# A third landing slot for the modulation blocks, and later first index scores, in a two-layer hybrid decoder trunk

## The chip, the cores and the metric

The kernel runs on one core of a Trainium2 chip. It is one hand-ordered program: every engine (TensorE = PE, VectorE = DVE, ScalarE = ACT, GpSimd = POOL, and SyncE = SP, which here issues nearly all DMAs) executes its own list of instructions in the order written, and semaphores tie the lists together. The metric is the device time of one execution in microseconds (us), lower is better.

## The reference

Two layers, 512 tokens (SEQ) of width 1024 (D). What matters for the change, cut to its core:

```python
c_act = silu(c)
for l in range(2):
    mod = c_act @ w_ada[l] + b_ada[l]                  # (1, 6144): six vectors of 1024
    sh1, sc1, gt1, sh2, sc2, gt2 = split(mod, 6)
    h = rmsnorm(x, g_norm1[l]) * (1 + sc1) + sh1
    proj = h @ w_in[l]                                 # 16 groups of columns, four attention groups A, B, C, D
    # group D: an indexer scores all keys for each query, the top 128 are attended
    #   score[q, k] = sum over 8 heads of wi[q, head] * relu(qi[q, head] . ki[k])
    x = x + gt1 * (four attentions @ w_out[l])
    h = rmsnorm(x, g_norm2[l]) * (1 + sc2) + sh2
    x = x + gt2 * mixture_of_experts(h)                # 16 experts, 2 per token
return rmsnorm(x, g_final)
```

All of it is float32. `w_ada[l]` is 1024 x 6144. Its first 2048 columns (sh1, sc1) are needed before the layer, the other 4096 (gt1, sh2, sc2, gt2) only after the attention.

## The kernel before, in words

**Modulation.** The 4096 later columns of `w_ada[l]` are read in 16 *blocks* of 128 rows x 2048 columns (1 MB), block b by `load_ada(b)` (L1485) on SP's queue into `ada_slot(b)` (L323), one of two slots at the end of `wbuf`, chosen by b % 2. DVE multiplies block b with one column of silu(c) and adds it to a running sum by `ada_step(b)` (L670; L675 for the first block of a sum, L678 for the others). Blocks 0 to 7 sum in `qB`, 8 to 15 in `kB`. `load_ada(b)` waits until DVE has used block b - 2. PE then adds the partitions up (`sum_mods`, L1091). In layer 0 blocks 16 to 23 follow during the output projection, for the next layer.

**Projection.** `w_in` comes in seven column *chunks* (CHUNKS, L32) through two slots of `wbuf`. Chunk n may be loaded (`load_in`, L1481) only when the last PE job that reads chunk n - 2 has filled its bank: chunk 2 waits for `kiwi`, chunk 3 for `kvD`, chunk 4 for `ckv`. A PE *job* is one output tile (8 matmuls of 512 columns; the profile counts 16 records for it) into one of six PSUM banks, taken round robin in the order of `plan` (L66). A job may begin when the bank's job six places earlier has been drained by ACT or DVE. Jobs of chunk 0 are qi0, qi1, kiwi, of chunk 1 qD0, qD1, kvD, of chunk 2 cq0, cq1, ckv, of chunk 3 qA0, qA1, kA0.

**Index scores.** The indexer runs for query tiles i = 1, 2, 3 (tile 0 needs none). For tile i, PE computes eight small products ("idx" jobs, `host`, L1144: four ahead of each of two projection jobs), ACT takes each through Relu into one of three `relu` buffers (`relus`, L495), DVE multiplies by `wi` and sums into `score` (`index_sums`, L723, L730 and L732), and `top(i)` (L736) takes the 128 largest in 16 rounds of MAX8 and MATCH_REPLACE8 and writes the mask `selmask`. The fourth Relu of a tile cannot run before DVE has consumed the first. Everything DVE does is in one order: blocks 0 to 9, `wi`, scores and top of tile 1, blocks 10 to 15, scores of tile 2, and so on.

**SP's order** in layer 0: chunk 1, blocks 0 and 1, five constant tables, blocks 2 and 3, the 17 small tables of the layer (`load_small`, L1420), blocks 4 to 8, chunk 2, blocks 9 to 11, chunk 3, blocks 12 to 15, chunks 4 to 6. Layer 1 has the same order without tables; its small tables were loaded in layer 0.

**Value tiles.** `vA`, `vB`, `vC`, `vD` (L157) hold the value rows of the attention groups. vA and vB are written from the jobs vA and vB on, well behind the last block of a layer.

## Time and profile before

| | us |
|---|---|
| median of 3 runs | 1188.87 (1188.62 to 1189.19) |
| the profiled execution | 1189.58, its span 1187.7 |
| PE busy | 1037.6 (87%) |
| DVE busy | 597.4 (50%) |
| ACT busy | 357.5 (30%) |
| DMA | 238.33 MB, mean 201 GB/s |

Read it in stages: in each of the two layers come projections with the indexer (about 39 to 216 us in layer 0, 616 to 785 us in layer 1), then attention, the output projection and the experts. The change touches only the first of these stages. A busy share of 87% for PE is an average; what a wait costs is read at its place. Times inside the trace count from the span's start; "clock" is the share of full speed that TensorE was granted.

### The profile page before, as it was taken

Reading aid. Unit: us, or ns where it says so; the run is one execution under the profiler, and the core shown is the slowest. Engines: PE = TensorE matmul, PEld = TensorE weight load, DVE = VectorE, ACT = ScalarE, POOL = GpSimd, SP = SyncE. Lnnn points to the kernel's source line nnn. Section 1 sums busy time; section 2 is a strip of 40 time slices with the busy share of each in tenths; the row PEclk is TensorE's granted clock in tenths of the full one; section 3 lists DMA queues with packets and bytes.
Section 4 is the critical chain, followed back from the end, with each engine's and each line's share of the span. In section 5 each row is a group of like instructions: output and inputs, shape, how many; then the busy total and the mean of one; then the engine's idle time right before and its main releaser. Section 6 shows DMA issues by size and latency. Waiting matters only on the chain.

```text
span 1187.7 us, 15253 instructions
## 1 busy us (share of the span) xinstructions
PE 1037.6 (87%) x5471; PEld 712.7 (60%) x5471; DVE 597.4 (50%) x1356; ACT 357.5 (30%) x809; POOL 94.3 (8%) x115
## 2 busy tenths in 40 slices
PE   3968999999997699999829899999999859999980
PEld 0423365788554687887624336568865558788860
DVE  1438688766555223223165769786732532322326
ACT  2121233666212223223032122366621222322312
POOL 3000102000000101000020010200000010110002
PEclk8888999999998699999959999999999969999995
DMA  9884425400246499999588451130000549999955
GB/s 364 267 286 146 171 73 172 201 1 1 106 160 222 109 353 360 372 370 356 192 290 295 165 196 54 36 142 1 1 1 36 178 141 348 356 377 369 354 192 212
DMA packets 141317, 238.33 MB, mean 201 GB/s; under 512 B 31322, under 2 KB 111690, under 8 KB 134990
## 3 DMA queue, kind: packets, MB, share of 16 engines
q1 hardware_dynamic: 134356, 212.52, 51.0%
q0 software_dynamic: 6912, 25.17, 5.7%
q8 instruction: 29, 0.48, 0.2%
q14 instruction: 20, 0.16, 0.0%
HBM read 214.57 MB, written 27.26 MB: 204 GB/s over the span
## 4 chain that ended last, share of the span: by engine, by line
PE 72%; DVE 11%; DMA 11%; issue 2%; SPq 2%; ACT 2%; POOL 1%; POOLq 0%; DVEq 0%; ACTq 0%
PE bank L1068 64%; DMA wbuf<-in_w_ada 7%; PE bank L1085 5%; PE bank L1353 2%; DMA bada<-in_b_ada 2%; DVE qB L678 2%; DVE tring L742 1%; DVE x L1046 1%; DVE kB L678 1%; DVE small L741 1%; DMA hT<-y_rows,ints 1%; DMA tok<-norm_rows,ints 1%; SPq L1449 1%; DVE tring L732 1%; DMA y_rows<-tok 1%
## 5 line engine op out<-in xcount | busy, mean ns | idle before, releaser
L1068 PE MATMUL bank<-hT,wbuf 128*128 128x128 f32 (+2 forms) x2560 | 463.1, 343 | 3.7 <-ACT pring L502 2.9
L1068 PEld LDWEIGHTS bank<-hT,wbuf 128*128 128x128 f32 (+1 forms) x2560 | 331.0, 194 | 137.3 <-issue 124.2
L1068 PE MATMUL bank<-wbuf,hT 128*128 128x512 f32 (+2 forms) x512 | 155.9, 462 | 1.4 <-ACT hT L474 1.4
L1068 PEld LDWEIGHTS bank<-wbuf,hT 128*128 128x128 f32 x512 | 86.5, 191 | 61.9 <-issue 56.4
L1018 DVE TENSOR_TENSOR tring<-bank,tring 128x256 f32<-128x256 f32 x32 | 13.6, 425 | 218.5 <-ACT tring L620 218.5
L1068 PE MATMUL bank<-wbuf,tring 128*128 128x512 f32 x256 | 114.8, 592 | 0.0
L564 ACT ACTIVATE tring<-tring,small 128x384 f32<-128x384 f32 (+5 forms) x128 | 69.3, 541 | 51.4 <-DVE small L813 50.0
L620 ACT ACTIVATE tring<-bank 128x256 f32<-128x256 f32 x32 | 12.3, 384 | 235.9 <-PE bank L1068 235.9
L1068 PEld LDWEIGHTS bank<-wbuf,tring 128*128 128x128 f32 x256 | 46.3, 190 | 46.9 <-issue 46.9
L1025 DVE TENSOR_TENSOR tok<-bank,gtB 128x512 f32<-128x512 f32 x64 | 44.3, 692 | 45.9 <-PE bank L1068 45.9
L678 DVE SCALAR_TENSOR_TENSOR qB<-wbuf,small,qB 128x2048 f32<-128x2048 f32 x21 | 49.3, 2350 | 25.7 <-DMA wbuf<-in_w_ada 25.3
L582 ACT ACTIVATE hT<-bank,modT,scaleT 128x128 f32<-128x128 f32 x128 | 48.3, 457 | 40.4 <-PE bank L1353 40.2
L1085 PE MATMUL bank<-ident,tring 128*128 128x128 f32 (+2 forms) x312 | 56.1, 273 | 1.3 <-ACT tring L564 1.3
L883 DVE TENSOR_SCALAR hT<-bank,scaleT,modT 128x128 f32<-128x128 f32 x128 | 43.7, 404 | 24.5 <-PE bank L1353 23.3
L741 DVE MAX8 small<-tring 128x8 f32<-128x256 f32 (+2 forms) x96 | 53.9, 561 | 3.3
L425 POOL COPY ints<-ints 128x1 int32 x32 | 5.9, 184 | 624.0 <-issue 387.5
L742 DVE MATCH_REPLACE8 tring<-small,tring 128x256 f32<-128x256 f32 (+2 forms) x96 | 52.0, 542 | 0.0
L1353 PE MATMUL bank<-ident,tok 128*128 128x128 f32 x256 | 36.8, 292 | 16.2 <-DMA tok<-norm_rows,ints 15.5
L1353 PEld LDWEIGHTS bank<-ident,tok 128*128 128x128 f32 x256 | 32.0, 151 | 24.7 <-issue 22.1
L1085 PE MATMUL bank<-ident,tok 128*128 128x128 f32 x128 | 18.8, 316 | 30.6 <-DVE tok L641 27.7
L678 DVE SCALAR_TENSOR_TENSOR kB<-wbuf,small,kB 128x2048 f32<-128x2048 f32 x14 | 32.9, 2352 | 23.6 <-DMA wbuf<-in_w_ada 23.4
L893 DVE TENSOR_TENSOR tring<-bank,gtB 128x512 f32<-128x512 f32 x16 | 11.1, 691 | 65.8 <-PE bank L1068 43.1
(236 smaller groups left out, 1185.9 us busy)
## 6 DMA issues: line engine op xcount, KB each, us to landing
wbuf<-in_w_ada SPq DMA_DIRECT2D x44, 1024.0 KB, 5.1
wbuf<-in_w_gate SPq DMA_DIRECT2D x32, 1024.0 KB, 6.9
wbuf<-in_w_up SPq DMA_DIRECT2D x32, 1024.0 KB, 9.2
wbuf<-in_w_down SPq DMA_DIRECT2D x32, 1024.0 KB, 9.1
y_rows<-tok SPq DMA_DIRECT2D x32, 512.0 KB, 9.6
wbuf<-in_w_in SPq DMA_DIRECT2D x8, 1536.0 KB, 6.5
wbuf<-in_w_out SPq DMA_DIRECT2D x2, 4096.0 KB, 13.8
y_rows<-in_k_zero SPq DMA_DIRECT2D x8, 512.0 KB, 7.3
```

Source lines behind the costliest of these rows:

```text
L564: nc.scalar.activation(t, t, ACT.Exp, bias=nmax[:, u:u + 1], scale=-1.0, accum_out=sums[:, u:u + 1]).then_inc(probs_ready, 1)
L582: return nc.scalar.activation(dst, src, ACT.Identity, bias=modT[:, 24 + k:25 + k], scale=scaleT[:, 8 + k:9 + k])
L620: nc.scalar.activation(sg[s], banks[2 + s][:, 0:256], ACT.Silu).then_inc(silu_ready[l], 1)
L678: nc.vector.scalar_tensor_tensor(out=total, in0=ada_slot(b), scalar=cact[:, k:k + 1], in1=total, op0=ALU.mult, op1=ALU.add).then_inc(ada_u ...
L741: link(nc.vector.max(max8, sc))
L742: link(nc.vector.match_replace(sc, max8, sc, TAKEN))
L883: return nc.vector.tensor_scalar(dst, src, scaleT[:, 8 + k:9 + k], modT[:, 24 + k:25 + k], ALU.mult, ALU.add)
L1018: nc.vector.tensor_tensor(hid[s], banks[2 + s][:, 256:512], sg[s], ALU.mult).then_inc(hidden_ready[l], 1)
L1025: nc.vector.tensor_tensor(ysb[s][:, m * 512:(m + 1) * 512], banks[4 + 2 * s + m][:, :], gtB[:, m * 512:(m + 1) * 512], ALU.mult).then_inc( ...
L1068: return nc.tensor.matmul(dst, lhsT, rhs, start=first, stop=last)
L1085: last = nc.tensor.transpose(dst, src, ident[0:size, 0:size])
L1353: last = nc.tensor.transpose(banks[half][:, k * P:(k + 1) * P], xg[s][:, (4 * half + k) * P:(4 * half + k + 1) * P], ident[:, :])
```

## The change

`vA` to `vD` become one tile `values`, whose first 2048 columns (vA and vB) serve as a third slot for blocks 2, 5, 8, 11 and 14 (`SLOT_OF`). `load_ada(b)` for b below 16 now waits for block b - 3. DVE does blocks 0 to 7, drains `wi`, does blocks 8 to 15, and only then the scores and top of tile 1. On PE and ACT the eight index products of tile 1 stand ahead of cq1 and ckv instead of qD1 and kvD. On SP, block 2 is loaded ahead of the constant tables and the layer's small tables go behind block 10.

```diff
--- before.py
+++ after.py
@@ -39,6 +39,8 @@
 
 ADA_SLOT = 2 * D
 ROUNDS = 3
+ADA_SLOTS = 3
+SLOT_OF = [b % 3 for b in range(2 * KT)] + [b % 2 for b in range(KT)]
 
 MAX_TILES = NE + 8
 OTHERS = MAX_TILES - NE
@@ -70,8 +72,8 @@
     jobs += [(("qD", 0), "act"), ("wiT", "dve")]
 
 
-    jobs += idx_jobs(1, ("qD", 1), "kvD")
-    jobs += [(("cq", 0), "act"), ("vDT", "act"), (("cq", 1), "act"), ("ckv", "act")]
+    idx1 = idx_jobs(1, ("cq", 1), "ckv")
+    jobs += [(("qD", 1), "act"), ("kvD", "act"), (("cq", 0), "act"), ("vDT", "act")] + idx1
     jobs += [("bias", "act")]
     idx2, idx3 = idx_jobs(2, ("qA", 0), ("qA", 1)), idx_jobs(3, ("kA", 1), ("qC", 0))
     jobs += idx2
@@ -154,7 +156,9 @@
     qB, kB = sb("qB", 4, SEQ), sb("kB", 4, SEQ)
     qC, kC = sb("qC", 4, SEQ), sb("kC", 2, SEQ)
     qD, kD = sb("qD", 4, SEQ), sb("kD", SEQ)
-    vA, vB, vC, vD = sb("vA", TT, 260), sb("vB", TT, 256), sb("vC", TT, 128), sb("vD", TT, 64)
+    values = sb("values", TT * (260 + 256 + 128 + 64))
+    vA, vB, vC, vD = [values[:, TT * at:TT * (at + w)].rearrange("p (i n) -> p i n", i=TT)
+                      for at, w in ((0, 260), (260, 256), (516, 128), (644, 64))]
     qi, ki = sb("qi", 2, SEQ), sb("ki", SEQ)
     tring = sb("tring", 4, SEQ)
     pring = sb("pring", 3, SEQ)
@@ -253,7 +257,7 @@
     fin_rows = sem("fin_rows")
     norm1_landed, scale1_ready = sem("norm1_landed"), sem("scale1_ready")
     small_landed, nsink_ready = sem("small_landed"), sem("nsink_ready")
-    ada_landed, ada_used = [sem(f"ada_landed{n}") for n in range(2)], sem("ada_used")
+    ada_landed, ada_used = [sem(f"ada_landed{n}") for n in range(ADA_SLOTS)], sem("ada_used")
     row_ready, sum_used = sem("row_ready"), sem("sum_used")
     win_landed = [sem(f"win_landed{n}") for n in range(len(CHUNKS))]
     rope_landed, wout_landed = sem("rope_landed"), sem("wout_landed")
@@ -321,8 +325,8 @@
         return wbuf[:, at:at + KT * cols].rearrange("p (k n) -> p k n", k=KT)
 
     def ada_slot(b):
-        at = KT * D + (b % 2) * ADA_SLOT
-        return wbuf[:, at:at + ADA_SLOT]
+        n = SLOT_OF[b]
+        return wbuf[:, KT * D + n * ADA_SLOT:KT * D + (n + 1) * ADA_SLOT] if n < 2 else values[:, 0:ADA_SLOT]
 
     def first_slot(k):
 
@@ -353,7 +357,7 @@
     CONSTS, SMALLS = 5, 15 + 2
 
     totals = {norm1_landed: 16, scale1_ready: 1, scale2_ready: 1, small_landed: SMALLS * 16, ada_used: ROUNDS * KT,
-              ada_landed[0]: ROUNDS * KT // 2 * 16, ada_landed[1]: ROUNDS * KT // 2 * 16, row_ready: ROUNDS, sum_used: ROUNDS, padded: 2,
+              row_ready: ROUNDS, sum_used: ROUNDS, padded: 2,
               rope_landed: 32, wout_landed: 16,
               squares_ready: TT, root_ready: 2 * TT, xhat_ready: TT, relu_used: 3 * IDX_HEADS, topk_done: 3,
               cq_squared: 3, latents_ready: 1, krope_ready: 2 + HEADS, qrope_ready: 1, nsink_ready: 1,
@@ -365,6 +369,8 @@
         totals[landed] = 32
     for landed in win_landed:
         totals[landed] = 16
+    for landed in ada_landed:
+        totals[landed] = SLOT_OF.count(ada_landed.index(landed)) * 16
     totals[win_landed[0]] = len(INDEX_PARTS) * 16
 
     def need(eng, signal, n):
@@ -509,14 +515,14 @@
                 drain("kiwi", (kiwiT[0:8, :], b[96:104, :]), *((ki[32 * r:32 * r + 32, :], b[0:32, :]) for r in range(4)),
                       (krT[0:32, :], b[32:64, :]), (krS[0:32, :], b[64:96, :]))
                 drain_pair(("qD", 0), qD, 0)
-                relus(1, 0)
                 drain_pair(("qD", 1), qD, 1)
-                relus(1, 4)
                 b = bank("kvD")
                 drain("kvD", (kD[0:64, :], b[0:64, :]), (vdT[0:64, :], b[64:128, :]))
                 drain(("cq", 0), (cqT[:, 0, :], bank(("cq", 0))[:, :]))
                 drain("vDT", (vD[:, :, :].rearrange("p i n -> p (i n)"), bank("vDT")[:, 0:256]))
+                relus(1, 0)
                 drain(("cq", 1), (cqT[:, 1, :], bank(("cq", 1))[:, :]))
+                relus(1, 4)
                 drain("ckv", (ckvT, bank("ckv")[:, :]))
                 need(act, small_landed, SMALLS * 16)
                 drain("bias", (biasT[:, :], bank("bias")[:, 0:48]))
@@ -669,7 +675,7 @@
                 norm_rows(i, i + 1, first_link, first_rows, first_root)
             def ada_step(b):
 
-                need(dve, ada_landed[b % 2], 16 * (b // 2 + 1))
+                need(dve, ada_landed[SLOT_OF[b]], 16 * (SLOT_OF[0:b].count(SLOT_OF[b]) + 1))
                 total, k = ada_sum[b // KT % 2], b % KT
                 if k == 0:
                     nc.vector.tensor_scalar(total, ada_slot(b), cact[:, 0:1], None, ALU.mult).then_inc(ada_used, 1)
@@ -712,7 +718,7 @@
                     wait_filled(dve, ("h1", k))
                     nc.vector.tensor_scalar(hT[:, k, :], bank(("h1", k))[:, :], scaleT[:, k:k + 1], modT[:, k:k + 1],
                                             ALU.mult, ALU.add).then_inc(dve_drained, 1)
-                for b in range(10):
+                for b in range(8):
                     ada_step(b)
                 wait_filled(dve, "wiT")
                 nc.vector.tensor_scalar(wi, bank("wiT")[:, 0:32].rearrange("p (i h) -> p i h", i=TT),
@@ -744,12 +750,12 @@
                         .then_inc(topk_done, 1)
                     need(dve, topk_done, i)
 
+                for b in range(8, 2 * KT):
+                    ada_step(b)
                 index_sums(1, 0)
                 index_sums(1, 4)
                 dve.wait_ge(consts_landed, CONSTS * 16)
                 top(1)
-                for b in range(10, 2 * KT):
-                    ada_step(b)
                 index_sums(2, 0)
                 index_sums(2, 4)
                 mod_row(0)
@@ -1150,15 +1156,15 @@
                             .then_inc(psum_filled, 1)
                     project(name, n, at, P)
 
-                host(("qD", 1), 1, P, 1, 0)
-                host("kvD", 1, 256, 1, 4)
+                project(("qD", 1), 1, P, P)
+                project("kvD", 1, 256, P)
 
                 need(pe, win_landed[2], 16)
                 project(("cq", 0), 2, 0, P)
                 wait_drained(pe, "kvD")
                 turn("vDT", [(bank("vDT")[:, i * 64:(i + 1) * 64], vdT[0:64, i * P:(i + 1) * P], 64) for i in range(TT)])
-                project(("cq", 1), 2, P, P)
-                project("ckv", 2, 256, P)
+                host(("cq", 1), 2, P, 1, 0)
+                host("ckv", 2, 256, 1, 4)
                 need(pe, small_landed, SMALLS * 16)
                 turn("bias", [(bank("bias")[:, 0:48], bada[0:48, :], 48)])
 
@@ -1483,28 +1489,27 @@
                     load_columns(l, n)
 
                 def load_ada(b):
-                    if b >= 2:
-                        need(sp, ada_used, b - 1)
+                    if b >= ADA_SLOTS:
+                        need(sp, ada_used, max(a for a in range(b) if SLOT_OF[a] == SLOT_OF[b]) + 1)
                     r, k = divmod(b, KT)
                     whose, at = (l, 2 * D + r * ADA_SLOT) if r < 2 else (l + 1, 0)
                     sp.dma_start(ada_slot(b), layer(whose, w_ada).rearrange("a k n -> (a k) n")[k * P:(k + 1) * P, at:at + ADA_SLOT])\
-                        .then_inc(ada_landed[b % 2], 16)
+                        .then_inc(ada_landed[SLOT_OF[b]], 16)
 
                 load_columns(l, 1)
                 load_ada(0)
                 load_ada(1)
+                load_ada(2)
                 if l == 0:
                     load_constants()
-                load_ada(2)
-                load_ada(3)
-                if l == 0:
-                    sp.wait_ge(first_turned, 1)
-                    load_small(0)
-                for b in range(4, 9):
+                for b in range(3, 9):
                     load_ada(b)
                 load_in(2)
                 load_ada(9)
                 load_ada(10)
+                if l == 0:
+                    sp.wait_ge(first_turned, 1)
+                    load_small(0)
                 load_ada(11)
                 load_in(3)
                 for b in range(12, 2 * KT):
```

The order of the instructions, before and after, at the places of interest. PE, the projection jobs between qD0 and the bias turn in layer 0 (`hT,wbuf x8` is one job, `ki,qi x4` four index products; `tring 128x8` is the turn wiT, `tring 128x64` the turn vDT), before:

```order
L1085 MATMUL bank<-ident,tring 128x8 x4
L1068 MATMUL bank<-ki,qi 128x256 x4
L1068 MATMUL bank<-hT,wbuf 128x512 x8
L1068 MATMUL bank<-ki,qi 128x256 x4
L1068 MATMUL bank<-hT,wbuf 128x512 x16
L1085 MATMUL bank<-ident,tring 128x64 x4
L1068 MATMUL bank<-hT,wbuf 128x512 x16
L1085 MATMUL bank<-ident,bada 128x48
```

The same stretch of PE in the changed kernel:

```order
L1091 MATMUL bank<-ident,tring 128x8 x4
L1074 MATMUL bank<-hT,wbuf 128x512 x24
L1091 MATMUL bank<-ident,tring 128x64 x4
L1074 MATMUL bank<-ki,qi 128x256 x4
L1074 MATMUL bank<-hT,wbuf 128x512 x8
L1074 MATMUL bank<-ki,qi 128x256 x4
L1074 MATMUL bank<-hT,wbuf 128x512 x8
L1091 MATMUL bank<-ident,bada 128x48
```

Three jobs (qD1, kvD, cq0) now follow wiT with nothing of the indexer between them; the index products stand around cq1. DVE, from the second running sum to the first scores in layer 0, before (L718 drains `wi`, L730 is the first score):

```order
L678 SCALAR_TENSOR_TENSOR qB<-wbuf,small,qB 128x2048 x7
L675 TENSOR_SCALAR kB<-wbuf,small 128x2048
L678 SCALAR_TENSOR_TENSOR kB<-wbuf,small,kB 128x2048
L718 TENSOR_SCALAR small<-bank 128x32
L730 TENSOR_SCALAR tring<-pring,small 128x256
L732 SCALAR_TENSOR_TENSOR tring<-pring,small,tring 128x256 x7
```

And in the changed kernel:

```order
L724 TENSOR_SCALAR small<-bank 128x32
L681 TENSOR_SCALAR kB<-values,small 128x2048
L684 SCALAR_TENSOR_TENSOR kB<-wbuf,small,kB 128x2048 x2
L684 SCALAR_TENSOR_TENSOR kB<-values,small,kB 128x2048
L684 SCALAR_TENSOR_TENSOR kB<-wbuf,small,kB 128x2048 x2
L684 SCALAR_TENSOR_TENSOR kB<-values,small,kB 128x2048
L684 SCALAR_TENSOR_TENSOR kB<-wbuf,small,kB 128x2048
L736 TENSOR_SCALAR tring<-pring,small 128x256
```

The whole second sum (8 blocks) now stands between `wi` and the first score; two of its blocks stood there before. SP around chunk 3 in layer 0 of the changed kernel (128x8x384 is a chunk, 128x2048 a block):

```order
L1448 DMA wk_n<-in_w_kv_up 128x4x64
L1449 DMA wk_v<-in_w_kv_up 128x4x64
L1496 DMA values<-in_w_ada 128x2048
L1417 DMA wbuf<-in_w_in 128x8x384
L1496 DMA wbuf<-in_w_ada 128x2048 x2
L1496 DMA values<-in_w_ada 128x2048
L1496 DMA wbuf<-in_w_ada 128x2048
L1417 DMA wbuf<-in_w_in 128x8x388
```

The small tables end just ahead of block 11, and blocks 12 to 15 stand behind chunk 3, as they did before.

## Rows read from the trace of the kernel before

**Rows 1.** The chain that ended last: start us, us, what; both layers.

```profile
80.58 9.11 DMA wbuf<-in_w_ada
...
125.33 5.05 DMA wbuf<-in_w_ada
...
133.72 40.80 PE bank L1068 x142
...
648.99 9.52 DMA wbuf<-in_w_ada
...
702.76 40.80 PE bank L1068 x142
```

**Rows 2.** PE in order of time, layer 0: start us, us, engine, line, tiles, [idle before].

```profile
69.58 0.20 PE L1085 MATMUL bank<-ident,tring 8*128 8x8 f32 x1
...
70.73 7.13 PE L1068 MATMUL bank<-hT,wbuf 128*128 128x512 f32 x16 [0.41 <-ACT qD L474]
92.22 1.24 PE L1068 MATMUL bank<-ki,qi 32*128 32x256 f32 x8 [14.35 <-DVE small L718]
93.39 16.26 PE L1068 MATMUL bank<-hT,wbuf 128*128 128x512 f32 x32
...
109.97 14.00 PE L1068 MATMUL bank<-hT,wbuf 128*128 128x512 f32 x32
...
133.72 7.13 PE L1068 MATMUL bank<-hT,wbuf 128*128 128x512 f32 x16 [0.78 <-ACT pring L502]
```

**Rows 3.** PE in order of time, layer 1.

```profile
649.24 0.20 PE L1085 MATMUL bank<-ident,tring 8*128 8x8 f32 x1
...
661.04 1.15 PE L1068 MATMUL bank<-ki,qi 32*128 32x256 f32 x8 [3.52 <-DVE small L718]
662.12 15.21 PE L1068 MATMUL bank<-hT,wbuf 128*128 128x512 f32 x32
...
702.76 7.13 PE L1068 MATMUL bank<-hT,wbuf 128*128 128x512 f32 x16 [2.14 <-ACT pring L502]
```

**Rows 4.** DVE in order of time, layer 0.

```profile
92.20 0.35 DVE L730 TENSOR_SCALAR tring<-pring,small 128x256 f32<-128x256 f32 x1
...
112.76 0.29 DVE L743 TENSOR_SCALAR selmask<-tring 128x256 f32<-128x256 f32 x1
...
132.67 0.41 DVE L730 TENSOR_SCALAR tring<-pring,small 128x384 f32<-128x384 f32 x1
...
141.98 0.69 DVE L684 COPY ada_row<-bank 128x512 f32<-128x512 f32 x1 [4.04 <-PE bank L1068]
```

**Rows 5.** ACT in order of time, layer 0.

```profile
92.64 0.39 ACT L502 ACTIVATE pring<-bank 128x256 f32<-128x256 f32 x1 [21.01 <-DVE tring L730]
```

**Rows 6.** SP's queue in order of time: first and last of the small tables.

```profile
51.75 0.43 SPq L1424 DMA_DIRECT2D bada<-in_b_ada  x1
...
61.77 0.64 SPq L1443 DMA_DIRECT2D wk_v<-in_w_kv_up  x1
```

**Rows 7.** DMAs to `wbuf` issued 69 to 72 us (block 6) by tile.

```profile
DMA to landing us min/median/max: 4.9/4.9/4.9
```

**Rows 8.** The same, 102 to 103.5 us: chunk 3 alone.

```profile
DMA to landing us min/median/max: 6.2/6.2/6.2
```

**Rows 9.** The same, 78.3 to 78.6 us: block 8, then chunk 2, layer 0.

```profile
L1490 SPq DMA_DIRECT2D wbuf<-in_w_ada x1: 328/328/328, 78.1 to 78.1; - x1
...
DMA to landing us min/median/max: 4.9/6.8/8.7
```

**Rows 10.** The same, 645.6 to 646.1 us: block 8, then chunk 2, layer 1.

```profile
L1411 SPq DMA_DIRECT2D wbuf<-in_w_in x1: 430/430/430, 645.8 to 645.8; - x1
DMA to landing us min/median/max: 5.0/6.9/8.8
```

**Rows 11.** Busy by stretch: us, busy PE, PEld, DVE, ACT, POOL, clock, DMA share, GB/s.

```profile
617.00:620.00 3.00, 3.00 (x16) 3.00 (x15) 1.61 (x2) 1.30 (x2) 0.00 (x0) 0.50 0.01 3
...
661.10:664.50 3.40, 3.40 (x11) 1.55 (x12) 2.71 (x7) 2.77 (x7) 0.00 (x0) 0.51 0.76 246
```

## The prediction

> **What bounds the kernel now.** I read the page first, then the chain of waits, then PE, DVE, ACT and SP in order of time over the first stage of both layers, and last each load's time to landing. The chain runs over PE for most of the span; where it leaves PE early in a layer it goes through modulation blocks and DVE, until it comes back to PE at 133.72 us in layer 0 and at 702.76 us in layer 1, both times at job qA1, and then stays on PE for 40.80 us [rows 1]. What happens ahead of qA1 counts in full, if qA1 moves; what is won elsewhere ahead of it counts nothing.
>
> Why does qA1 start there? In layer 0 PE stands still for 14.35 us from 77.87 us, because an index product wants a bank that DVE must drain (`wi`, L718), and DVE is busy with blocks 0 to 9 [rows 2]. Only then (92.20 us) come the scores of tile 1, the top of tile 1 (its mask written at 112.76 + 0.29 = 113.05 us), blocks 10 to 15, and at 132.67 us the first score of tile 2 [rows 4]. That score frees a `relu` buffer, ACT fills it, the bank of idx(2, 3) is free and qA1 starts 1.05 us later. So DVE sets qA1, and DVE waits for blocks. In layer 1 the same pattern has a stall of 3.52 us and one of 2.14 us [rows 3].
>
> **Step 1, the early jobs (PE).** With the index products gone from ahead of qD1 and kvD, both follow the wiT turn, which ends at 69.58 + 0.20 = 69.78 us in layer 0 and 649.24 + 0.20 = 649.44 us in layer 1 [rows 2, 3]. Two jobs take 14.0 us (the row at 109.97 us) [rows 2]. With 0.1 us of handover kvD is full at K = 83.9 us in layer 0 and 663.5 us in layer 1. K matters, since chunk 3 may only be loaded then, and blocks 12 to 15 stand behind it in SP's one queue, which the order of SP shows. That is the new wait: behind the waiting chunk stand four blocks, and for them waits DVE.
>
> **Step 2, blocks 0 to 11 (three slots).** One block alone lands 4.9 us after its issue [rows 7]. Queued ones follow closer: block 8 lands at 78.1 + 4.9 = 83.0 us, chunk 2 at 78.5 + 8.7 = 87.2, block 9 at 80.58 + 9.11 = 89.7 [rows 1, 9], so 4.2 us for a chunk and 2.5 for a block. DVE takes 2.35 us for a block (L678 on the page). With three slots a block is issued while two others are summed (4.7 us), so the blocks come at about 2.5 us each. From the first use at 46.5 us in layer 0 blocks 0 to 7 end near 67 us and DVE then waits for wiT (69.8). Blocks 9 and 10 are behind chunk 2, near 76 us. The small tables take SP from 51.75 to 62.4 us, 10.7 us [rows 6]; now from about 67 to 78 us. Block 11 then lands near 83 and is used by 86 us, before anything behind K can come. Blocks 0 to 11 are hidden in both layers, by PE's work up to K; in layer 1 all are used near 659 us. If that cover were gone, every us of delay beyond K + 9 would be a us at qA1.
>
> **Step 3, behind K (SP, DMA, DVE).** Chunk 3 alone lands in 6.2 us [rows 8], at K + 6.3. Blocks 12, 13 and 14 are issued at once and land at K + 8.8, 11.2 and 13.7; block 15 needs the slot of block 12 (used by K + 11.2) and lands 4.9 us later, K + 16.1. DVE is done at K + 18.5. Scores plus top of tile 1 took 113.05 - 92.20 = 20.85 us [rows 4]; 0.5 of it was a wait for ACT behind the qD1 drain, whose place a shorter drain takes, so 20.3. Then 1.05 to qA1: K + 39.9. That is 123.8 us in layer 0 (9.9 earlier than 133.72) and 703.4 us in layer 1 (0.6 later than 702.76). Sum: -9.3 us.
>
> Layer 1 gains nothing, since its stall at 657.5 was short, DVE was at its first score at 661.0, and the new order puts six more blocks ahead of that score and chunk 3 ahead of four of them.
>
> The trace knows one slower delivery: in layer 1 chunk 2 landed at 645.8 + 8.8 = 654.6 [rows 10], and block 9 at 648.99 + 9.52 = 658.5 [rows 1], 3.9 us behind it and not 2.5. Bounds per layer: 0 and 1.4 us. I take half of one such case over both layers, +0.7.
>
> The page "SBUF — State Buffer" of the Trainium skill (The DMA setup-cost knee) gives a transfer about 2 us plus its bytes at 436 GB/s: an estimate by it is 5.6 us for the chunk and 2.4 more for each block, DVE done at K + 17.7, and the total 1.6 us lower. The rows measured 6.2 and 4.9 us where it gives 5.6 and 4.4, so the rows decide.
>
> **Step 4, PE behind the first score.** PE does cq0, cq1 and then cannot start ckv, whose bank is that of idx(1, 3), the fourth Relu. That Relu ran 0.83 us after the first score began (92.64 + 0.39 - 92.20 [rows 4, 5]), so ckv starts at K + 19.4, after a stall of about 5 us (14.35 before in layer 0, 3.52 in layer 1). Two jobs and three short groups (some 16.0 us) take it to K + 35.4, where it waits for qA1 again.
>
> Every stall has a second price. After 3.52 us of standing, the clock was 0.51 over the next 3.4 us [rows 11], the lower of its two levels (1.2 GHz), and kvD and cq0 took 15.21 us instead of 14.0 [rows 2, 3]; with the small products 1.5 us. After 14.35 us it was 16.26 us, and 2.6 us with the products. After 2.14 us (702.76) a job took the full-speed 7.13 us. The slow stretch behind the 5 us stall (1.5 to 2.6 us) lies ahead of DVE's chain and is hidden; it shortens the second stall to 39.9 - 35.4 - 2 = 2.5 us, between 2.14 (no price) and 3.52 (a price). Bounds 0 and 1.5 per layer; I take one of the two, +1.5. It counts, since DVE's next step waits for PE's sums behind qA1 (4.04 us of idle at 141.98 [rows 4]).
>
> The page "TensorE: Matmul & The Clock Gate" of the Trainium skill (What's actually happening) says that the gate keeps its own time, not the kernel's. By that rule a 2.5 us stall can cost in one layer and not in the other. The trace agrees in so far as stalls of 2.14 and 3.52 us differ; no run here shows one length both ways.
>
> **Step 5, everything else.** From qA1 on, PE and DVE have their old order, and what they wait for hangs on their own jobs: chunk 4 is issued when ckv is full, some 12 us earlier in layer 0, with its first job 20 us after qA1. The third slot adds 1 MB to the load ahead of layer 1. It queues behind blocks 0 and 1, and the DMA share falls to 0.01 by 617 us [rows 11], while DVE wants block 2 only at 625.7: nothing. The gathers at the layer's end use another queue and are finished by then. vA and vB are written after block 15 by more than 25 us. The constant tables, one block later, are wanted at about 108 us. No instruction is added or removed in these parts.
>
> **The sum.** -9.3 + 0.7 + 1.5 = -7.1 us. The profiled execution took 1189.58 us (span 1187.7, 1.9 around it), 0.7 above the median of the runs, 1188.87; applied to that, 1181.8 us.
>
> **The rivals.** *A, delivery behind chunk 3 is slow.* The four blocks come at the spacing s that makes four steps in each of two layers, so every us above 2.45 costs 8 us in all. At 3.9 us, seen once, that is +11.6 on -7.8 (the sum without the 0.7): 1192.7 us, slower than before. If the loads did not overlap at all (4.9 us each) it would be 1200.7. It decides from s = 3.4 on. For it: the landing 3.9 us behind chunk 2, the one place where a block waited behind a chunk in layer 1. Against it: 2.5 us at the same place in layer 0, and chunk 3 finds an empty queue.
>
> *B, something holds chunk 3 back in layer 0.* It is issued in SP's order behind the small tables and block 11. If the tables take 7 us more than the 10.7 before, being now queued behind blocks 9 and 10, chunk 3 goes out 2 us after K and block 11 is late too; price 3 to 4 us, 1185.5 us. For it: loads of many small pieces. Against it: they took 10.7 us where blocks 2 and 3 were ahead of them too.
>
> *C, the clock.* Both second stalls fall at the lower level for as long as after 14.35 us, 2.6 us each: -9.3 + 0.7 + 5.2 = -3.4, 1185.5 us; with K 0.5 us late in both, 1186.5. Against it: the stall is under 3 us.
>
> **How the numbers follow.** Forecast 0.70, A 0.12, B 0.08, C 0.10. The likeliest's own range is 1178 (no clock price, the faster delivery, and 1.6 us quicker than summed) to 1185.4 (both clock prices, 1.4 late in both layers). The range 1178 to 1187 takes in B and C and leaves out most of A. About 0.2% (2.4 us) is what a measurement can tell from no change. Faster by more: 0.69 of the forecast, 0.03 of A, 0.05 of B, 0.06 of C, less 0.03 for what I don't see: 0.80. Slower by more: 0.07 of A and 0.01: 0.08. Within: 0.12.
>
> **What would show it.** qD1 and kvD back to back behind wiT, kvD full near 83.9 and 663.5 us; L736 (the first score) near 102.4 and 682.0; stalls of about 5 and 2.5 us in both layers instead of 14.35 in one; qA1 near 123.8 and 703.4; from there to attention the same distance as before. It is wrong if block 15 is used later than K + 20, if block 11 is not used before K + 8 in layer 0, if the clock is low behind both second stalls, or if qA1 moves and the attention's start does not.

## The result and the profile after

| | before | after |
|---|---|---|
| median, us | 1188.87 (5 runs, 1188.62 to 1189.91) | 1193.83 (5 runs, 1193.11 to 1196.13) |
| profiled execution, us | 1189.58, span 1187.7 | 1193.11, span 1191.3 |
| ratio, 95% interval | | 1.0036 [1.0023, 1.0049] |

The change makes the kernel slower by 0.36%, clear of its interval. 1181.8 us was forecast, so the direction was wrong too. On other chips and at other hours the kernel before has medians of 1188.4 to 1190.8 us, so kernels are compared below by their ratio to the kernel before, run beside them on the same chip. Two executions far off all others, one of the kernel before (2239.52 us) and one of a1 below (3828.29 us), are left out of the ratios.

PE in order of time in the changed kernel, layer 0 (three early jobs; ckv; qA0; qA1; the first attention scores), then layer 1 (the same without qA0). These rows answer to [rows 2, 3]:

```profile
68.57 20.87 PE L1074 MATMUL bank<-hT,wbuf 128*128 128x512 f32 x48
...
107.90 9.54 PE L1074 MATMUL bank<-hT,wbuf 128*128 128x512 f32 x16 [9.72 <-ACT pring L508]
...
129.29 8.83 PE L1074 MATMUL bank<-hT,wbuf 128*128 128x512 f32 x16 [2.88 <-ACT pring L508]
...
214.15 0.91 PE L1074 MATMUL bank<-kA,qA 128*128 128x128 f32 x6 [1.06 <-DVE modT L694]
...
647.07 20.87 PE L1074 MATMUL bank<-hT,wbuf 128*128 128x512 f32 x48
...
681.79 9.32 PE L1074 MATMUL bank<-hT,wbuf 128*128 128x512 f32 x16 [5.10 <-ACT pring L508]
...
703.18 8.83 PE L1074 MATMUL bank<-hT,wbuf 128*128 128x512 f32 x16 [3.11 <-ACT pring L508]
...
787.93 0.91 PE L1074 MATMUL bank<-kA,qA 128*128 128x128 f32 x6 [0.94 <-DVE modT L694]
```

The early jobs do run back to back. But PE now stands still twice in each layer, for 9.72 and 2.88 us and for 5.10 and 3.11 us, and behind each stall a job takes 8.8 to 9.5 us in place of 7.13. The attention scores began at 216.73 and 785.78 us in the trace before:

```profile
216.73 0.91 PE L1068 MATMUL bank<-kA,qA 128*128 128x128 f32 x6 [0.91 <-DVE modT L688]
...
785.78 0.91 PE L1068 MATMUL bank<-kA,qA 128*128 128x128 f32 x6 [0.91 <-DVE modT L688]
```

So layer 0 won 2.6 us up to there, and layer 1, which began 2.3 us ahead, came out 2.15 us behind: it lost 4.5 us. The rest, from 2.15 to the 3.6 us between the spans of the two profiled executions, comes behind attention (last part).

DVE in order of time in the changed kernel, from block 9 to the first score of tile 1 and of tile 2, in layer 0 and, from block 12 on, in layer 1; they answer to [rows 4]:

```profile
75.61 2.35 DVE L684 SCALAR_TENSOR_TENSOR kB<-wbuf,small,kB 128x2048 f32<-128x2048 f32 x1 [5.32 <-DMA wbuf<-in_w_ada]
78.53 2.35 DVE L684 SCALAR_TENSOR_TENSOR kB<-wbuf,small,kB 128x2048 f32<-128x2048 f32 x1 [0.57 <-DMA wbuf<-in_w_ada]
89.40 2.35 DVE L684 SCALAR_TENSOR_TENSOR kB<-values,small,kB 128x2048 f32<-128x2048 f32 x1 [8.51 <-DMA values<-in_w_ada]
95.76 4.84 DVE L684 SCALAR_TENSOR_TENSOR kB<-wbuf,small,kB 128x2048 f32<-128x2048 f32 x2 [4.02 <-DMA wbuf<-in_w_ada]
...
104.75 2.35 DVE L684 SCALAR_TENSOR_TENSOR kB<-wbuf,small,kB 128x2048 f32<-128x2048 f32 x1 [1.66 <-DMA wbuf<-in_w_ada]
107.02 0.35 DVE L736 TENSOR_SCALAR tring<-pring,small 128x256 f32<-128x256 f32 x1
...
128.24 0.42 DVE L736 TENSOR_SCALAR tring<-pring,small 128x384 f32<-128x384 f32 x1
...
669.94 4.82 DVE L684 SCALAR_TENSOR_TENSOR kB<-wbuf,small,kB 128x2048 f32<-128x2048 f32 x2 [12.21 <-DMA wbuf<-in_w_ada]
...
678.64 2.35 DVE L684 SCALAR_TENSOR_TENSOR kB<-wbuf,small,kB 128x2048 f32<-128x2048 f32 x1 [1.39 <-DMA wbuf<-in_w_ada]
680.91 0.35 DVE L736 TENSOR_SCALAR tring<-pring,small 128x256 f32<-128x256 f32 x1
```

Read the brackets: between `wi` and the first score DVE waits for blocks for 5.32 + 0.57 + 8.51 + 4.02 + 1.66 = 20.1 us in layer 0, and in layer 1 once for 12.21 us, with three short waits beside it (0.48, 1.41 and 1.39 us). The first score comes 14.8 us later than before in layer 0 (92.20) and 19.9 us later in layer 1 (661.02), and 21.2 us of DVE's work (scores and top of tile 1, from 107.02 to the first score of tile 2 at 128.24) stand between it and qA1.

SP's queue in order of time, layer 0, from the fourth small table to block 15, and chunk 3 in layer 1; they answer to [rows 6]:

```profile
70.60 4.36 SPq L1438 DMA_DIRECT2D vecT<-in_g_q_mla  x1
...
82.68 0.63 SPq L1449 DMA_DIRECT2D wk_v<-in_w_kv_up  x1
...
84.69 0.43 SPq L1417 DMA_DIRECT2D wbuf<-in_w_in  x1
...
91.78 0.33 SPq L1496 DMA_DIRECT2D values<-in_w_ada  x1
98.14 0.33 SPq L1496 DMA_DIRECT2D wbuf<-in_w_ada  x1
...
661.11 0.38 SPq L1417 DMA_DIRECT2D wbuf<-in_w_in  x1
```

One table's issue took 4.36 us, and all 17 took SP from 69.2 to 83.3 us, 14.1 us and not 10.7. Chunk 3 goes out at 84.69 us, 2.1 us after kvD was full (82.6), and block 11 lands just before its use at 89.40.

### The profile page after: what moved, and what is told of

It reads as the page before. It is cut to its first block, busy times and chain, and to the rows that moved or that the text cites. A ratio compares the mean times of both kernels' runs of the same rounds, so it can differ in the third digit from the quotient of the medians.

```text
span 1191.3 us, 15255 instructions
## 1 busy us (share of the span) xinstructions
PE 1043.6 (88%) x5471; PEld 715.9 (60%) x5471; DVE 599.0 (50%) x1356; ACT 357.1 (30%) x809; POOL 92.2 (8%) x115
## 4 chain that ended last, share of the span: by engine, by line
PE 73%; DVE 12%; DMA 9%; SPq 2%; issue 2%; ACT 2%; POOL 0%; POOLq 0%; DVEq 0%; ACTq 0%
PE bank L1074 65%; PE bank L1091 5%; DMA wbuf<-in_w_ada 5%; PE bank L1359 3%; DVE tring L748 2%; DVE small L747 2%; DMA bada<-in_b_ada 2%; DVE x L1052 1%; DMA hT<-y_rows,ints 1%; DVE tring L738 1%; DMA tok<-norm_rows,ints 1%; SPq L1455 1%; DVE qB L684 1%; DMA y_rows<-tok 1%; SPq L1438 1%
## 5 line engine op out<-in xcount | busy, mean ns | idle before, releaser
L1074 PEld LDWEIGHTS bank<-values,pring 128*128 128x128 f32 x592 | 82.9, 191 | 21.6 <-issue 11.5
L1074 PE MATMUL bank<-values,pring 128*128 128x64 f32 x592 | 80.6, 265 | 0.0
## 6 DMA issues: line engine op xcount, KB each, us to landing
y_rows<-tok SPq DMA_DIRECT2D x32, 512.0 KB, 10.2
```

Of the source, the lines that this page charges most:

```text
L1074: return nc.tensor.matmul(dst, lhsT, rhs, start=first, stop=last)
```

## The experiments

In the list of versions, "old order" means two things: on PE and ACT the index products stand ahead of qD1 and kvD, and DVE does blocks 0 to 9 ahead of tile 1; "new order" is the change's. The eleven versions that ran and the change itself, by ratio to the kernel before:

| version | slots | order | small tables behind | ratio | 95% |
|---|---|---|---|---|---|
| the change | 3 | new | block 10 | 1.0036 | 1.0023 to 1.0049 |
| e1 | 3 | new | block 3 | 1.0026 | 1.0013 to 1.0038 |
| a1 | 2 | new | block 10 | 1.0092 | 1.0071 to 1.0112 |
| b1 | 3 | old | block 3 | 0.9884 | 0.9866 to 0.9902 |
| b2 | 2 | old | block 10 | 0.9930 | 0.9913 to 0.9948 |
| c1 | 3 | old | block 10 | 0.9795 | 0.9779 to 0.9811 |
| c2 | 3 | old | chunk 3 | 0.9809 | 0.9782 to 0.9836 |
| d1 | 3 | products new, DVE old | block 10 | 1.0130 | 1.0113 to 1.0147 |
| e3 | 3 | new, stall filled | block 10 | 0.9987 | 0.9976 to 0.9998 |
| e2 | 3 | new, chunk 3 behind block 15 | block 10 | 0.9945 | 0.9930 to 0.9961 |
| e4 | 3 | as e2 | chunk 3 | 0.9882 | 0.9868 to 0.9897 |
| a2 | 3 | as e4, products ahead of cq0, cq1 | chunk 3 | 0.9857 | 0.9830 to 0.9885 |

My first theory after the result was that the queue (the tables and chunk 3's wait) lost what was forecast. The runs e1 to e4 tested it.

**e1, the tables back behind block 3.**

```diff
-                for b in range(3, 9):
+                load_ada(3)
+                if l == 0:
+                    sp.wait_ge(first_turned, 1)
+                    load_small(0)
+                for b in range(4, 9):
                     load_ada(b)
...
-                if l == 0:
-                    sp.wait_ge(first_turned, 1)
-                    load_small(0)
```

> The changed kernel with one part undone: the 17 small tables stand behind block 3 again. Theory (the tables hold SP until 84.7 us in layer 0, so chunk 3 goes out 2 us late and block 11 lands at 89.4 us, which delays blocks 14 and 15): chunk 3 is issued within 0.3 us of kvD, the first score of tile 1 comes 19.9 us after kvD is full as in layer 1 and not 24.4, near 102.5 us, and the time falls by 4.6 us to about 1189.2. Rival (blocks behind a chunk come slowly wherever the tables are): first score still near 107 us, time within 1 us of 1193.8.

Measured: 1193.61 us, ratio 1.0026, and the first score at 107.42 us. The theory falls and the rival holds. Chunk 3 was issued at 82.75 us, nearly at once, but DVE in this kernel waits where the tables now stand (8.37 us ahead of block 4), and block 9 comes 10.6 us later than in the change:

```profile
67.25 2.35 DVE L684 SCALAR_TENSOR_TENSOR qB<-wbuf,small,qB 128x2048 f32<-128x2048 f32 x1 [8.37 <-DMA wbuf<-in_w_ada]
...
86.20 4.83 DVE L684 SCALAR_TENSOR_TENSOR kB<-wbuf,small,kB 128x2048 f32<-128x2048 f32 x2 [5.24 <-DMA wbuf<-in_w_ada]
```

With sixteen blocks ahead of the first score, every piece of the queue is ahead of it, and where the tables stand among them moved it by only 0.4 us.

**e2, chunk 3 issued behind block 15.**

```diff
                 load_ada(11)
-                load_in(3)
                 for b in range(12, 2 * KT):
                     load_ada(b)
+                load_in(3)
```

> The changed kernel with chunk 3 issued behind block 15 instead of ahead of block 12; tables as in the change. Theory (the wait of chunk 3 for kvD is what holds blocks 12 to 15 and with them DVE and qA1): layer 1's idle of DVE ahead of block 12 (12.21 us) goes, its first score comes near 667 us, not 680.9, its PE stalls of 5.10 and 3.11 us vanish; layer 0 gains some 5.5 us; together 1193.8 - 12.6 - 1.7 - 5.5 = about 1174. Rival (DMA throughput bounds the blocks, chunk 3 only takes its turn): DVE's last block moves by no more than the 4.2 us of a chunk in each layer, about 1185; and qA0 may then wait for chunk 3.

Measured: 1184.28 us, ratio 0.9945; against the change 0.9945 / 1.0036 = 0.991, 10.8 us. Layer 1's wait of 12.21 us went, as expected, and the last block of layer 1 was used 14.9 us earlier (by 666.1 and not 681.0; 1.9 of it because the layer began earlier). Yet only half of the 20 us forecast came. In layer 0 the tables still stood ahead of block 11, which was used by 93.6 us: the first score came only 1.4 us earlier (105.62 us) and not 5.5. In layer 1 the reason is in DVE's rows of this kernel: the scores of tile 1 now wait for ACT, for 1.47 and 5.68 us, and the first of tile 2 follows 26.7 us behind the first of tile 1, not 21.2.

```profile
667.53 0.54 DVE L736 TENSOR_SCALAR tring<-pring,small 128x256 f32<-128x256 f32 x1 [1.47 <-ACT pring L508]
...
675.31 2.44 DVE L738 SCALAR_TENSOR_TENSOR tring<-pring,small,tring 128x256 f32<-128x256 f32 x4 [5.68 <-ACT pring L508]
...
694.19 0.42 DVE L736 TENSOR_SCALAR tring<-pring,small 128x384 f32<-128x384 f32 x1
```

The products themselves were late: the second four stand behind cq1 on PE, which ends at 674.2 us. With the queue out of the way, the new order on PE sets the pace of tile 1 in layer 1, and PE stands 4.41 us ahead of qA1 there.

**e3, the stall ahead of qA1 filled.**

```diff
-                host(("qA", 1), 3, P, 2, 4)
...
+                for _ in range(3):
+                    mm(banks[7][:, :], ones[:, :], hT[:, 0, :])
+                project(("qA", 1), 3, P, P)
```

> The changed kernel with three extra full matmuls (128x512, result unused, some 2.6 us of PE time) behind the last index product of tile 2, in the stall ahead of qA1 (2.88 and 3.11 us in the trace). Theory (that stall lowers the clock and makes qA1 take 8.83 us in place of 7.13): qA1 takes 7.13 us in both layers, time falls by 2 x 1.7 = 3.4 us to about 1190.4. Rival (the lower clock comes from the earlier, longer stall or from elsewhere): qA1 stays at 8.83 us and the time stays at 1193.8, or rises if the added matmuls outlast the stall.

Measured: 1188.17 us, ratio 0.9987; against the change 0.995, 5.8 us. PE in this kernel at qA1, layer 0 and layer 1:

```profile
126.78 2.84 PE L1074 MATMUL bank<-hT,ones 128*128 128x512 f32 x6
130.07 7.13 PE L1074 MATMUL bank<-hT,wbuf 128*128 128x512 f32 x16 [0.45 <-ACT pring L508]
...
700.42 7.13 PE L1074 MATMUL bank<-hT,wbuf 128*128 128x512 f32 x16 [0.61 <-ACT pring L508]
```

Three matmuls of no use make qA1 take 7.13 us again: the lower clock was the price of a stall of 2.9 and 3.1 us, 1.7 us each. That is 3.4 of the 5.8 us. In layer 0 qA1 also began 0.78 us later than in the change (130.07 for 129.29), behind blocks that landed later. Most of the rest lies in code that e3 does not touch, where the lower clock happened to end sooner: the rise where the experts begin came 2.3 us sooner behind PE's restart in each layer, worth some 1.1 us each time, and layer 1's first turns took 5.16 us and not 5.90 (last part).

**e4, blocks, then chunk 3, then the tables.** The edit is e2's, and `load_small(0)` behind `load_in(3)`.

> The changed kernel with both: SP issues blocks 9 to 15, then chunk 3, then the small tables. Theory: layer 0's blocks come at 2.5 us each from 75.6 us on, last one used by about 93.5, qA1 near 115 us instead of 129.3 (133.7 before the change); layer 1 as in the kernel with chunk 3 last, PE-bound, qA1 near 690; in all about 1160 us. Rival (throughput): about 1180. A third way: the late tables hold PE at the bias turn, which stands behind ckv near 105 us, if they land after that.

Measured: 1176.31 us, ratio 0.9882. Of the 34 us expected 18 came. DVE used block 15 of layer 0 by 99.0 us and not by 93.5; qA1 in layer 1 stood 4.41 us for the late products, as in e2. Also the third way was there, small: the bias turn waited 1.48 us for the last table.

The theory now was another: not the queue but the new order itself loses, and the slot and the tables' place are gains. The next runs took the change apart.

**b1, the third slot alone** (all of `values`, `SLOT_OF` and the waits of `load_ada`; every order as before).

> The kernel before with the third slot alone; every order stays as it was (blocks 0 to 9, scores and top of tile 1, blocks 10 to 15). Theory (the third slot is the good part of the change, the new order of the scores the bad one): DVE reaches the first score some 3.5 us earlier in layer 0 and some 7 us earlier in layer 1, blocks 10 to 12 are there when top of tile 1 ends, so the six blocks take 15 us and not 19.6; qA1 some 8 us earlier in layer 0 and, PE-bound, 6 to 7 us in layer 1: 1189 - 14 = about 1175. Rival (loads are bound by throughput, a third slot changes little): within 2 us of 1189.

Measured: 1176.88 us, ratio 0.9884, close to the 1175 expected. DVE of this kernel, blocks 10 to 15 behind tile 1, layer 0:

```profile
108.94 2.35 DVE L684 SCALAR_TENSOR_TENSOR kB<-wbuf,small,kB 128x2048 f32<-128x2048 f32 x1
111.39 2.35 DVE L684 SCALAR_TENSOR_TENSOR kB<-values,small,kB 128x2048 f32<-128x2048 f32 x1
113.85 5.40 DVE L684 SCALAR_TENSOR_TENSOR kB<-wbuf,small,kB 128x2048 f32<-128x2048 f32 x2
119.35 2.35 DVE L684 SCALAR_TENSOR_TENSOR kB<-values,small,kB 128x2048 f32<-128x2048 f32 x1
121.81 2.94 DVE L684 SCALAR_TENSOR_TENSOR kB<-wbuf,small,kB 128x2048 f32<-128x2048 f32 x1
```

No bracket: the six blocks take 15.8 us and wait for nothing, while before they took 19.6 (from 113.09 to 132.67). Top of tile 1 is the cover under which they and chunk 3 land. The new order takes that cover away: it wants all sixteen blocks before tile 1 begins.

**b2, the tables behind block 10 alone.**

```diff
                 load_ada(3)
-                if l == 0:
-                    sp.wait_ge(first_turned, 1)
-                    load_small(0)
                 for b in range(4, 9):
                     load_ada(b)
                 load_in(2)
                 load_ada(9)
                 load_ada(10)
+                if l == 0:
+                    sp.wait_ge(first_turned, 1)
+                    load_small(0)
                 load_ada(11)
```

> The kernel before with the small tables behind block 10 alone. Theory (in layer 0 the tables hold SP for 10.7 us and whatever stands behind them): blocks 4 to 9 are no longer held, the first score of tile 1 comes near 80 us instead of 92.2, PE's stall of 14.35 us shrinks to some 2 us, qA1 comes near 122 and not 133.7: about 1177. Rival (the tables cost the same 10.7 us wherever they stand, as in the run with them early, where the first score moved from 107.0 to 107.4): 1189. Layer 1 is the same in both.

Measured: 1182.14 us, ratio 0.9930. The first score came at 85.7 us, not at 80: with two slots blocks 4 to 8 still take some 3.7 us each (first uses from 61.87 to 76.53 us), and PE's stall shrank to 8.29 us and not to 2. The theory's direction holds: half of it at the first score and some two thirds of it in the time (0.70%, 8 us, of the 12 expected).

**a1, the change with two slots** (`SLOT_OF = [b % 2 ...]`, `ADA_SLOTS = 2`, block 2 behind the constants).

> The changed kernel with the third slot undone. Theory (with 8 blocks ahead of the first score the third slot is needed): in layer 1 block 14 waits for block 12's use, the first score comes 21 us after kvD and not 19.9; in layer 0 blocks 0 to 10 take 3.7 us each, so that tables, block 11 and chunk 3 come some 4 us later: about 1199. Rival (chunk 3's wait sets everything, the slots nothing): 1194 to 1195.

Measured: 1201.21 us, ratio 1.0092, 1199 expected. The slot is worth 0.56% in the new order and 1.16% in the old.

**a2, e4 with the products ahead of cq0 and cq1** (in `plan`, ACT's drains and PE's `host` calls alike).

> The kernel with blocks, chunk 3, tables in that order (1176.3), and besides the eight index products of tile 1 ahead of cq0 and cq1 instead of cq1 and ckv. In that kernel's layer 1 the second four products stood behind cq1 (674 us relative to its own start at 635), so that the scores of tile 1 took 26.7 us to the first score of tile 2 and not 21.2, and PE stood 4.4 us ahead of qA1. Theory: this wait of DVE for ACT goes, the stall ahead of qA1 in layer 1 falls below 1 us with its clock price (9.8 us for qA1 in place of 7.13), layer 0 stays, since blocks bound it there: about 1169 to 1171. Rival (blocks bound layer 1 as well): within 1 us of 1176.

Measured: 1173.13 us, ratio 0.9857, its interval overlapping with e4's (0.9882): by the medians 3 us, with six runs spread from 1167.61 to 1176.61. In the trace qA1 of layer 1 has no stall and takes 7.13 us, as the theory says; the gain by the medians is half of it, and that remains unclear.

**c1, the change without its new order** (third slot, tables behind block 10).

> The kernel before with the third slot and with the small tables behind block 10: the change without its new order of scores and index products (and with block 2 behind the constant tables). Theory (both parts are gains and the new order alone is the loss): block 9 lands near 75.6 us, the first score comes near 78 us, PE's stall ahead of the index products (11.13 us with the third slot alone) falls below 1 us, PE runs through to qA1 near 115 us and layer 1 is as with the third slot alone: about 1164, so that the new order costs some 30 us. Rival (tables cost layer 0 what they save, since chunk 3 and blocks 11 to 15 queue behind them): 1175 to 1177, as with the third slot alone.

Measured: 1164.25 us, ratio 0.9795 [0.9779, 0.9811], as the theory says. This is the run that decides: the same slot and the same queue as in the change but for block 2 behind the constant tables, the old order on PE, ACT and DVE, and 1.0036 / 0.9795 = 1.025, or 29 us, between them. PE of this kernel from the index products to qA1, layer 0:

```profile
78.72 0.71 PE L1074 MATMUL bank<-ki,qi 32*128 32x256 f32 x8 [1.48 <-DVE small L724]
79.59 15.70 PE L1074 MATMUL bank<-hT,wbuf 128*128 128x512 f32 x32
...
118.50 7.13 PE L1074 MATMUL bank<-hT,wbuf 128*128 128x512 f32 x16
```

And busy time by stretch in the same kernel (us, then PE, weight loads, DVE, ACT, POOL, the clock, DMA share, GB/s), from qD1 to qA1 in layer 0, then in layer 1:

```profile
70.00:118.50 48.50, 46.76 (x125) 19.88 (x125) 39.71 (x71) 9.77 (x26) 5.84 (x3) 0.96 0.77 257
632.90:677.80 44.90, 44.89 (x125) 19.31 (x125) 38.33 (x70) 9.77 (x25) 6.03 (x3) 1.00 0.56 212
```

PE is busy for 46.76 of 48.50 us and for 44.89 of 44.90: in this stage the kernel is bound by PE. Of the two stalls that the change set out from, the one of 14.35 us is down to 1.48 us and the one of 3.52 us is gone, without moving a product.

**c2, the tables behind chunk 3, old order.**

> The kernel before with the third slot and with the small tables behind chunk 3, that is ahead of block 12 while DVE is in top of tile 1. Theory (tables should go where DVE has no want of a block): block 11 is there early, blocks 12 to 15 are issued near 97 us and still come in time, PE has no stall in either layer; same as the kernel with tables behind block 10 or 1 to 3 us better, 1161 to 1164. Rival (blocks 12 to 15 come late behind the tables): qA1 waits, 1168 or more.

Measured: 1164.22 us, ratio 0.9809 [0.9782, 0.9836]: the same as c1, and no rival at work. The 3 us better, the upper end of the expectation, did not come; PE bounds both. The two traces differ in one thing. Ahead of the index products PE stands 1.88 us here and 1.48 us in c1, and the two jobs behind them take 14.00 us here and 15.70 us in c1 (last part):

```profile
78.68 0.71 PE L1074 MATMUL bank<-ki,qi 32*128 32x256 f32 x8 [1.88 <-DVE small L724]
79.54 14.00 PE L1074 MATMUL bank<-hT,wbuf 128*128 128x512 f32 x32 [0.15 <-ACT pring L508]
```

**d1, the products late alone** (c1 with the change's order on PE and ACT, DVE as before).

> The changed kernel with DVE's order undone (blocks 0 to 9, scores and top of tile 1, blocks 10 to 15) but the index products still ahead of cq1 and ckv; against the kernel with third slot and tables (1164.3) it moves the products alone. Theory (the new order loses because the tile 1 work of 20 us on DVE starts late, whichever engine is the cause; the products late are enough): DVE waits for products that PE computes near 90 and 98 us in layer 0, and 21 and 28 us behind wiT in layer 1, top of tile 1 ends near 115.5 us, six blocks take 15 us, qA1 comes near 132 us in layer 0 (118.5 with the products early) and some 18 us later in layer 1, each with up to 2.6 us of lower clock: 1195 to 1200. Rival (only DVE's eight blocks ahead of the first score, with chunk 3 ahead of four of them, cost the time; products late cost nothing): 1164 to 1168.

Measured: 1205.44 us, ratio 1.0130, some 5 us above the 1195 to 1200 expected. Moving eight small products (0.71 us for four) behind other jobs costs 3.4% against c1. DVE of this kernel at tile 1, layer 0, and PE at the first six records of qA1, layer 1:

```profile
90.90 0.36 DVE L736 TENSOR_SCALAR tring<-pring,small 128x256 f32<-128x256 f32 x1 [11.75 <-ACT pring L508]
...
98.61 2.45 DVE L738 SCALAR_TENSOR_TENSOR tring<-pring,small,tring 128x256 f32<-128x256 f32 x4 [5.79 <-ACT pring L508]
```

```profile
715.00 5.41 PE L1074 MATMUL bank<-hT,wbuf 128*128 128x512 f32 x6 [18.94 <-ACT pring L508]
```

DVE waits 11.75 and 5.79 us for products, and PE waits 18.94 us for DVE ahead of qA1 in layer 1. So products late are enough to lose all of the gain and more. Once they are late, DVE does better to sum blocks in that gap: from d1 to the change the ratio falls from 1.0130 to 1.0036 (block 2's place moved too).

That does not clear the other half of the new order, DVE's sixteen blocks ahead of tile 1. In the changed kernel itself DVE waits, up to the first score, for blocks and for no product: the first four products are done at 90.5 us and the last four at 98.2, and the first score comes at 107.02, right behind block 15. By these rows it would have come no earlier with the products where they were, as long as all sixteen blocks stand ahead of it. So in the change DVE's order holds tile 1 back, and with that undone the products do (d1); the gain comes only when both are undone (c1). The fourth combination, products early and all blocks first, was not run, and what it costs is argued from these rows and not shown.

## Why the prediction was wrong, by its steps

**The bound** was read rightly: qA1 is where the chain enters PE, and DVE's tile 1 with its 20 us stands ahead of it. In both traces the distance from qA1 to attention is PE's own (83.0 us before in both layers; 84.9 and 84.8 after, of which 1.7 is the clock).

**Step 1** held: kvD is full at 82.6 and 661.0 us (83.9 and 663.5 forecast; relative to wiT the same). PE's four first jobs took 27.63 us in layer 0 where they had taken 29.17: from 40.0 to 43.5 us the granted clock was 1.00, and 0.52 before. That was luck, since their order and the idle time ahead of them (1.49 us) are the same in both.

**Step 2** failed in layer 0, at its sentence that blocks 0 to 11 are hidden. The tables took 14.1 us and not 10.7, and block 11 was used by 91.8 us (K + 9.2) and not by 86. Block 14 needs its slot and was issued at 91.78, block 15 at 98.14.

**Step 3** is the step that failed: the time from K to DVE's last block. DVE was forecast to end block 15 at K + 18.5. It ended at K + 24.4 in layer 0 and K + 19.9 in layer 1. Its tile 1 up to qA1 took 22.3 us and not 21.4: the half us of waiting for ACT did not go away, and the seven sums behind the first took 4.41 us, waits included, where they had taken 4.07. Landing times of the queue in the changed kernel, chunk 3 in layer 0, then chunk 3 and block 15 in layer 1:

```profile
L1417 SPq DMA_DIRECT2D wbuf<-in_w_in x1: 434/434/434, 84.7 to 84.7; - x1
DMA to landing us min/median/max: 8.6/8.6/8.6
...
L1417 SPq DMA_DIRECT2D wbuf<-in_w_in x1: 383/383/383, 661.1 to 661.1; - x1
DMA to landing us min/median/max: 6.3/6.3/6.3
...
L1496 SPq DMA_DIRECT2D wbuf<-in_w_ada x1: 328/328/328, 672.3 to 672.3; - x1
DMA to landing us min/median/max: 6.3/6.3/6.3
```

In layer 1 chunk 3 and block 12 came as summed (6.3 us; first use at K + 8.9 for 8.8), and blocks 12 to 14 at 2.4 us each; only block 15 took 6.3 us against 4.9 [rows 7], which is the whole 1.4 us there. It was not alone as in those rows: issued at 672.3, it had block 14 ahead of it until 674.8 and landed 3.8 us behind it. In layer 0 three terms make up the 5.9 us, to 0.3. Chunk 3 was issued 2.1 us late; it took 8.6 us to land and not 6.2, with block 11 issued 1.3 us ahead of it; and block 15 took 6.6 us and not 4.9, landing 4.0 us behind block 14. So rival A (slow delivery) was there for one block a layer, and rival B (chunk 3 held back by the tables) was there with the 2 us it named and 2.4 us more of landing. But e1 shows that B was no separate fault that could be mended by moving the tables.

Three of the four signs that the prediction named for being wrong came: block 15 later than K + 20 (in layer 0), block 11 used later than K + 8 in layer 0 (by K + 9.2), and the lower clock behind both second stalls.

**Step 4**: the first stall was 5.10 us in layer 1, as forecast, and 9.72 us in layer 0, where about 5 was forecast, because of step 3. Both second stalls fell on the costly side, 2.88 and 3.11 us with 1.7 us each, where one was taken at 1.5. e3 shows it. That is rival C, at 1.7 and not 2.6 us each.

**In numbers**: layer 0 was forecast at -9.9 for qA1 and came at -4.4 (129.29 for 133.72), +5.5: K was 1.3 us earlier, block 15 came 5.9 later behind it and tile 1 took 0.9 more. Layer 1 was forecast at +0.6 and its qA1 came, against its own start 2.3 us earlier, at +2.7, +2.1. The clock at the two places cost 3.4 and not 1.5, +1.9. Behind attention +1.4 where 0 was summed, less 0.7 taken for slow delivery, which is contained in the first two. Together 10.2 of the 10.7 us between -7.1 and the +3.6 of the profiled executions.

**What lay below it**: the sum took the change as one path and asked only whether that path was shorter than the old one. It never asked what each part was worth alone. The two good parts (third slot 0.9884, tables 0.9930, together 0.9795) are worth 24 us, more than the whole forecast, and the new order costs 29 us on top. A hint was in the rows: DVE's top of tile 1 is 20 us in which nobody wants a block, and blocks 10 to 15 with chunk 3 could land under it [rows 4].

## What to carry to other kernels

When a change bundles a resource (a slot, a shorter queue) with a new order, price each alone before the sum: the order may spend more than the resource earns. A long piece of work on one engine that needs little from a busy queue is the cover for that queue; put it as early as its inputs allow, and put small products that feed it ahead of large jobs, however small they are. The best kernel here, with c2 no different, is the old order with the third slot and the tables behind block 10, 1164.25 us, 2.05% faster than before [0.9779, 0.9811].

## What the runs showed of the hardware

The stalls of 2.9 and 3.1 us in the changed kernel cost more than their length: with the array at its lower level behind them, 16 records took 8.83 us and not 7.13, and three useless matmuls in the stall gave the 1.7 us back.

But the length of a stall alone does not say whether it has this price. Behind 1.48 us of standing in c1 the granted clock was 0.50 from 80.0 to 82.8 us; behind 1.88 us at the same place in c2 it was 1.00. In the kernel before 2.14 us had no price. The prediction looked for the border between 2.14 and 3.52 us and said that no run showed one length both ways; 1.49 us ahead of layer 0's first jobs does (0.52 before, 1.00 after).

What was behind the attention moved as well, with no instruction changed there. Clock in the changed kernel where the experts of layer 1 begin (us, busy PE, weight loads, DVE, ACT, POOL, clock, DMA share, GB/s):

```profile
972.00:974.00 2.00, 2.00 (x11) 2.00 (x10) 1.01 (x4) 1.85 (x5) 1.09 (x2) 0.50 0.00 0
974.00:976.00 2.00, 2.00 (x12) 2.00 (x11) 0.35 (x2) 0.93 (x1) 0.63 (x2) 0.50 0.69 211
976.00:978.00 2.00, 2.00 (x18) 2.00 (x18) 0.00 (x0) 0.00 (x0) 0.51 (x1) 0.91 0.50 150
```

And in the kernel before:

```profile
969.00:971.00 2.00, 1.94 (x9) 1.98 (x10) 0.62 (x2) 0.82 (x3) 0.36 (x2) 0.50 0.00 0
971.00:973.00 2.00, 2.00 (x16) 2.00 (x16) 1.37 (x4) 1.97 (x3) 0.97 (x2) 0.80 0.25 53
```

PE takes up its turns there again at 970.98 us after and at 969.06 before, 1.9 us apart, and the clock rises near 976.4 and 971.8, 4.6 us apart; the stretch at the lower clock is longer by 2.7 us, which costs some 1.3 us. The same instructions had their rise 5.4 us behind the restart in one trace and 2.7 us in the other. The page "TensorE: Matmul & The Clock Gate" of the Trainium skill (What's actually happening) says that the gate's window runs free and does not reset when a kernel starts, so that the point of the rise varies, and these two traces agree. It limits what a time can tell here: e3 gained 2.4 us beyond its cause, and whether a2 lost some that way is not shown. What makes block 15 take 6.3 to 6.6 us to land, 3.8 to 4.0 us behind block 14 and not 2.4, stays open.
